# A two-layer decoder trunk on one core: the gate block's second conv tap two chunks later, the shared parts of the value block one chunk sooner

## The reference

```python
D_MODEL = 2048; SEQ = 256; D_FF = 11 * D_MODEL // 4; FFN_CONV = 3     # D_FF = 5632

def conv_ffn(h, w_up, conv_w, conv_b, w_down):
    u = causal_dwconv(h @ w_up, conv_w, conv_b)      # width 3, over the tokens, each channel by itself
    gate, val = jnp.split(u, 2, axis=-1)
    return (jax.nn.gelu(gate) * val) @ w_down

for l in range(DEPTH):                               # DEPTH = 2
    x = x + mixer_l(rmsnorm(x, norm_mix[l]))
    x = x + conv_ffn(rmsnorm(x, norm_ffn[l]), ffn_w_up[l], ffn_conv_w[l], ffn_conv_b[l], ffn_w_down[l])
```

## Time and profile before

| | |
|---|---|
| median of 3 runs | 2173.3 us (2173.15 to 2174.23) |
| profiled execution, its own time | 2177.84 us |
| its span in the profile | 2176.1 us |
| busy: TensorE, DVE, ACT | 100%, 78%, 63% |
| granted TensorE clock | 1.0 |
| DMA | 230 GB/s in the mean |

### The profile page before, as it was taken

One profiled execution on the slowest core, in us unless ns is written; L12 is line 12 of the kernel. 1 busy time (PEld: TensorE's weight loads), 2 busy tenths in 40 slices (PEclk: granted clock), 3 DMA queues, 4 the chain that ended last, 5 costly groups with the idle time before them and its releaser, 6 DMA issues.

```text
span 2176.1 us, 28498 instructions
## 1 busy us (share of the span) xinstructions
PE 2167.0 (100%) x9780; PEld 1795.9 (83%) x9780; DVE 1706.7 (78%) x1968; ACT 1360.0 (63%) x1950; POOL 16.6 (1%) x48
## 2 busy tenths in 40 slices
PE   9999999999999999999999999999999999999999
PEld 8888888887888888888888888888888888888887
DVE  7877866788888887887776676577888888878875
ACT  6654445677777777655555555556777777766553
POOL 2000000000000000000000000000000000000000
PEclk9999999999999999999999999999999999999999
DMA  8666667777777787666676777567877787777774
GB/s 276 218 210 211 200 191 242 218 236 239 246 248 239 245 253 237 208 223 213 228 245 201 233 263 242 186 220 217 257 229 253 229 255 232 257 237 217 238 246 156
DMA packets 269357, 500.15 MB, mean 230 GB/s; under 512 B 18928, under 2 KB 56832, under 8 KB 269136
## 3 DMA queue, kind: packets, MB, share of 16 engines
q1 hardware_dynamic: 267408, 492.78, 71.3%
q0 software_dynamic: 1424, 5.60, 0.7%
q10 hardware_dynamic: 432, 0.56, 0.1%
HBM read 457.15 MB, written 41.71 MB: 229 GB/s over the span
## 4 chain that ended last, share of the span: by engine, by line
PE 82%; DVE 7%; DMA 4%; ACT 3%; issue 3%; SPq 0%; ACTq 0%; DVEq 0%
PE ps L1186 16%; PE ps L1188 16%; PE ps L1187 16%; PE ps L1081 7%; PE ps L1083 7%; PE ps L1082 7%; PE ps L1058 4%; DMA h<-turn_line 2%; PE ps L1092 2%; PE ps L1094 2%; PE ps L1093 2%; DVE w_lo L1419 2%; PE ps L1062 2%; ACT w_hi L620 1%; DMA raw<-w_down 1%
## 5 line engine op out<-in xcount | busy, mean ns | idle before, releaser
L1419 DVE TENSOR_TENSOR w_lo<-raw,w_hi 128x1024 fp32r<-128x1024 f32 x744 | 897.9, 1222 | 347.2 <-ACT w_hi L620 334.6
L620 ACT ACTIVATE w_hi<-raw 128x1024 fp32r<-128x1024 f32 x744 | 770.9, 1053 | 441.4 <-PE ps L1188 165.2
L1186 PE MATMUL ps<-w_hi,xs 128*128 128x512 f32 x1904 | 743.2, 390 | 0.3 <-DVE w_lo L1419 0.3
L1187 PE MATMUL ps<-w_lo,xs 128*128 128x512 f32 x1904 | 740.8, 389 | 0.0
L1188 PE MATMUL ps<-w_hi,xs 128*128 128x512 f32 x1904 | 740.8, 389 | 0.0
L1186 PEld LDWEIGHTS ps<-w_hi,xs 128*128 128x128 f32 x1904 | 357.4, 188 | 75.7 <-DVE w_lo L1419 2.1
L1188 PEld LDWEIGHTS ps<-w_hi,xs 128*128 128x128 f32 x1904 | 357.4, 188 | 74.6
L1187 PEld LDWEIGHTS ps<-w_lo,xs 128*128 128x128 f32 x1904 | 357.5, 188 | 73.5
L1081 PE MATMUL ps<-w_hi,act 128*128 128x512 f32 x736 | 286.9, 390 | 0.4 <-DVE w_lo L1419 0.2
L1082 PE MATMUL ps<-w_lo,act 128*128 128x512 f32 x736 | 286.4, 389 | 0.0
L1083 PE MATMUL ps<-w_hi,act 128*128 128x512 f32 x736 | 286.4, 389 | 0.0
(11 more groups left out here) (312 smaller groups left out, 2004.8 us busy)
## 6 DMA issues: line engine op xcount, KB each, us to landing
raw<-w_up SPq DMA_DIRECT2D x352, 512.0 KB, 4.4
raw<-w_in SPq DMA_DIRECT2D x191, 512.0 KB, 4.5
raw<-w_down SPq DMA_DIRECT2D x176, 512.0 KB, 4.8
turn_line<-cross SPq DMA_DIRECT2D x284, 128.0 KB, 2.4
h<-turn_line SPq DMA_DIRECT2D x71, 512.0 KB, 5.3
raw<-w_out SPq DMA_DIRECT2D x64, 512.0 KB, 4.8
prob_line<-probs_t SPq DMA_DIRECT2D x12, 192.0 KB, 3.7
probs<-prob_line SPq DMA_DIRECT2D x3, 768.0 KB, 6.3
```

What stands on the lines that cost most here:

```text
L620: act_f(w_hi[:, s, :, :], raw[:, s, :, :], ACT.Copy).then_inc(hi_ready, 1)
L1186: mm(out, x_hi, w_hi[:, s, u, :], start=first and u == 0 and not (begun and t == 0), stop=False)
L1187: mm(out, x_hi, w_lo[:, s, u, :], start=False, stop=False)
L1419: tt(w_lo[:, s, :, :], raw[:, s, :, :], w_hi[:, s, :, :].bitcast(F32), ALU.subtract).then_inc(lo_ready, 1)
```

## The change

The second tap add of a gate block (L1844) moves from stage 14 to stage 16, that is from behind chunk 6 to behind chunk 8 of the next pair, and its GELU from stage 15 to stage 17, behind chunk 9. The first tap add stays at stage 13. For the value block nothing moves but the last `up_add`, which goes from behind chunk 4 to behind chunk 3 of the next pair. The stages from 16 on are called behind chunks 8 to 15, for the gate block alone.

```diff
-UP_FOLD_AT = (11, 12, 4)
+UP_FOLD_AT = (11, 12, 3)
+TAP_ADDS, GELU_AT = ((13, 16), (13, 14)), 17
...
                 else:
+                    mlp_post(2 * KC + c, ph, 0, j - 1, fast_last)
                     mlp_post(KC + c, ph, 1, j - 1, fast_last)
                     mlp_post(c, ph, 0, j, fast)
...
-            if stage == 15 and half == 0:
+            if stage == GELU_AT and half == 0:
                 eng.wait_ge(conv_done, k + 1)
                 act_f(pad_g[:, :, 0:S], pad_g[:, :, 0:S], ACT.Gelu_apprx_tanh).then_inc(gelu_done, 1)
...
                 else:
+                    mlp_post(2 * KC + c, ph, 0, j - 1)
                     mlp_post(KC + c, ph, 1, j - 1)
                     mlp_post(c, ph, 0, j)
...
-            if stage == 13:
+            if stage == TAP_ADDS[half][0]:
...
-            if stage == 14:
+            if stage == TAP_ADDS[half][1]:
```

## The result

The changed kernel takes 2186.56 us (median of 4 runs, 2185.54 to 2190.78), the kernel before beside it 2173.49 us (2173.15 to 2174.23). The ratio is 1.0063, 95% interval 1.0046 to 1.0081: 13.1 us or 0.63% slower. The forecast was 2185.3 us. The span of the profiled execution grew from 2176.1 to 2189.0 us, 12.9 us, with the same instructions. All lines of the changed kernel are 1 to 3 higher: L1092 is L1094, L1419 is L1421, L1782 is L1784, L1844 is L1847, L774 is L776.

What follows compares the result with a forecast made beforehand. TensorE's 42.84 us pair was the floor, beside an about equally long loop of `h` fetches, ACT and DVE. Per layer 8.8 us, less 1.4, 1.1, 0.6, plus 0.6, rounded to 6; 12 us on 2173.3 gave 2185.3 us, range 2174 to 2202.

Steps and rivals of the forecast that it cites:

- The loop: Value-block fetch, ACT's taps, DVE, gate-block fetch, taps, DVE and back: about one TensorE pair, a late microsecond not given back.
- step b: Gate's second tap add from chunk 6 to 8: both `up_lo` end 1.34 us sooner, margin from 0 to 1.3 us.
- step a: Shared parts added to the value block at chunk 3 instead of 4, in DVE's idle time: gain 0.
- step c: What waits for the moved add: SP's value-block fetch goes 2.6 us later, GELU on ACT from 656.38 to 660.4.
- The fetch takes 3.7 us, the loop grows by 1.1 us.: Value-block fetch on emptier queue takes 3.7 us instead of 5.1; taps start at 664.4; loop 1.1 us longer, 8 per layer.
- The fetch lands in 3.2 us: Sign that the forecast is wrong: value block's fetch landing 3.2 us after issue, where 3.7 was expected.
- the second rival: Value-block fetch comes so early that ACT's readiness leads: 0.6 us later on average, 2176.7 us, no change; chance 0.20.
- Load 12 behind the fetch: In SP's queue behind the value block's fetch: goes at 660.9, its chunk is used at 672.1, costs nothing.
- The small terms: Per layer: 1.4, 1.1 and 0.6 us off, 0.6 us on top for chunk 15 in the last fast pair.
- The terms taken off: Per layer: 1.4 us for shortened long fetches, 1.1 us chunk 6's margin, 0.6 us slack at gate block's arrival.
- stalls at chunks 6, 15 and 0 and a pair of 43.9 us: Expected on PE: waits on `w_lo` of chunks 6 and 15 or 0, pair 43.9 us; wrong if 43.1.
- the third rival: TensorE, not the loop, keeps the pace and only `up_lo` margin was missing: 5.7 us go, 2167.6 us; chance 0.07.

## Why the prediction came true, and where it was off

**The loop**. Shown for a late fetch: one that is late by one load without any other edit costs 40 us over 16 loops, and the pairs are longer by what ACT waits. That the loop and not TensorE keeps the pace of the kernel before is not shown. The two are nearly equal there: a fetch sent 1.5 us sooner gained nothing, though a load then took its place, and with one add less every pair takes TensorE's 42.84 us.

**Relief at `up_lo`** (step b). Right in kind: the waits are gone and both `up_lo` end early. In size it was 5.7 us at most in the profiled execution, and the forecast had not taken it as a gain. Measured by leaving the add out, it is 1.5 us.

**Shared parts at chunk 3** (step a). Forecast 0, measured ratio 1.0002.

**The fetch leaves 2.6 us later** (step c). Measured 2.54 us.

**The fetch takes 3.7 us, the loop grows by 1.1 us.** The term is mis-sized: it takes 3.1 to 3.4 us, and ACT reaches the taps at that moment, 0.7 us later than before in the pair shown and 0.4 in the mean of the loop's pairs. "The fetch lands in 3.2 us" was one of the forecast's own signs of being wrong, and it came. By this alone the second rival's 2176.7 us would have come; the kernel with half of load 12, at 1.0020 of the kernel before or 2177.8 us, is near it. The row I took the value from the earlier trace rows had loads that were still landing when the fetch was issued at 1205.38: the later of the two, sent at 1200.8, took 7.0 us. The Trainium skill's sum ("DMA: Bandwidth & Descriptors", section "Anatomy of one DMA"), an estimate of 3.2 us, agrees with the 3.2 us in the trace once the queue is empty, though the page gives the sum for transfers issued from GpSimd, and this one is issued from SP.

**Load 12 behind the fetch: "Nothing."** This step failed. I had compared its landing with TensorE's use of chunk 12 and not with ACT's, which is 7 us sooner (`w_hi` 12 starts at 665.2 in the kernel before, the matmuls at 672.1), and had let it take 3.6 us as before. It took 4.3 to 6.3 us. The half load says that this is about 9 of the 13 us, and so do the waits in the changed kernel's own trace, 9.1 us. So the two wrong terms, a fetch too slow by 0.5 us and a load that costs nothing, nearly cancel. That the 12 us of the forecast are right in sum is luck; right by reasoning is what sets them off (the wait for `conv_done` that holds up SP's queue), but about two thirds of the cost pass through another transfer than the one I named. The warning stood in the trace of the kernel before. This load left 0.39 us behind the very fetch from which I took the 3.7 us:

```profile
raw<-w_in SPq DMA_DIRECT2D x1, 512.0 KB, 5.3
```

**The small terms.** Behind the last fast pair 0.6 us a layer were forecast on top; 1.3 us were lost. The terms taken off (1.4, 1.1 and 0.6 us a layer) weren't measured one by one.

**Where it shows.** Forecast were stalls at chunks 6, 15 and 0 and a pair of 43.9 us; the stalls are there, and the pairs are 43.6 and 44.1 us. ACT's idle time ahead of the value block's taps was forecast as some 0.5 us each; the view of waits has 0.5 us in all.

**Faster, the third rival**, is refuted by two runs: without the add the gain is 1.5 us, and the late fetch alone costs 40.

**Left open:** why layer 1 loses 10.4 us and layer 0 5.7 in the changed kernel. The waits say where: 5.1 against 4.0 us for load 12, and 5.3 against 2.2 us for the gate block's fetch. With half of load 12 the latter are 2.2 us in both layers, which lose 3.6 and 3.7 us. That points at load 12 once more, but each is one execution, and how the load would reach the other fetch isn't shown. A second `h`, which would let the fetch go without waiting for `conv_done`, wasn't tried.

## What to carry to other kernels

A step that is moved out of a crowded place takes its signal along: look who waits for that signal, and above all what stands behind the waiting instruction in an in-order DMA queue. A transfer has to be compared with its first reader, here ACT's rounding of the chunk, not with the engine that multiplies it four chunks later. Before hunting stalls in a trace, compare the profiled execution's time with the median: of the 5.7 us seen here, in an execution 4.5 us above the median, 1.5 us were there to be won by times, 3.7 at most.

## What the runs showed of the hardware

A load of 512 KB took 3.5 to 4.3 us in 14 of 16 pairs when it left 2.8 us behind a fetch of 512 KB, and 4.6 and 5.1 us in the other two (kernel before). Close behind one it took longer: 4.4 to 5.7 us at 0.9 us behind (the kernel with the fetch one load earlier), 4.3 to 6.3 us at 0.4 to 0.6 us behind (changed kernel), though the loads ahead of the fetch had landed before it left; halved, it took 3.2 to 3.8 us. The fetch took 3.1 to 3.4 us with no load in the 4.4 us ahead, 4.4 to 5.2 us with one 1.1 us ahead in one kernel (load 12 first) and 3.8 to 5.3 us in another (fetch one load earlier), and 5.0 to 6.6 us with loads 2.5 and 0.6 us ahead (5.1 in the earlier trace rows). So of two such transfers issued within about a microsecond the second was late, whichever it was; in the kernel before they are 2.8 us apart, by where the waits happened to lie.
